# A feed-forward stage with two loading buffers of its own, gate weights loaded singly, and a new order of its first requests

## The reference

```python
def conv_ffn(x, w_up, conv_w, conv_b, w_down):
    h = x @ w_up                                  # 1024 -> 2 * 2816
    h = causal depthwise conv of width 3 over positions, + conv_b
    val, gate = jnp.split(h, 2, axis=-1)
    return (jax.nn.gelu(gate) * val) @ w_down     # 2816 -> 1024
# h = h + conv_ffn(rms_norm(h, norm_ffn_g), ...)
# gate = sigmoid(rms_norm(h, norm_ple_g) @ ple_w_gate)
# h = h + gate * (p @ ple_w_proj);  out = rms_norm(h, final_norm_g)
```

## Time and profile before

| What | Value |
|---|---|
| Median of 3 runs | 2889.82 us (2889.08 to 2893.59) |
| Profiled execution, its own time | 2886.86 us |
| Its span | 2885.3 us |
| Mean granted clock of TensorE | 0.955 of full speed |
| Feed-forward stage | about 1177 to 2605 us of the span |
| First half: up, down | about 1226 to 1659 us, 1659 to 1922 us |
| Second half: up, down | about 1922 to 2346 us, 2346 to 2605 us |

### The profile page before, as it was taken

How to read it: one execution, slowest core, us unless ns; L and a number is a source line. 1 busy time by engine, 2 the same in 40 slices (tenths; PEclk the granted TensorE clock), 3 DMA queues, 4 the chain that set the end, 5 groups by cost and what they waited for, 6 DMA issues and landing times. The chain is left out here.

```text
span 2885.3 us, 38789 instructions
## 1 busy us (share of the span) xinstructions
PE 2607.5 (90%) x13883; PEld 2239.3 (78%) x13883; DVE 1712.4 (59%) x3358; ACT 1368.2 (47%) x2460; POOL 509.6 (18%) x309
## 2 busy tenths in 40 slices
PE   6999997999845799489999999999999998997998
PEld 5989986999834588478888777778888876775876
DVE  1110272777596776488888755578888864444333
ACT  3343332666423666455555444455555542334444
POOL 3454454666300121000000000000000000000000
PEclk9999998999977799789999999999999999998999
DMA  4665456888333253312222366642222246662221
GB/s 163 195 213 172 152 170 157 188 185 185 70 100 126 87 182 129 104 59 88 88 81 75 116 208 232 224 146 88 88 81 75 87 152 245 223 205 99 79 76 46
DMA packets 313909, 392.09 MB, mean 136 GB/s; under 512 B 22161, under 2 KB 222161, under 8 KB 310650
## 3 DMA queue, kind: packets, MB, share of 16 engines
q1 hardware_dynamic: 299850, 341.60, 39.2%
q0 software_dynamic: 13888, 48.25, 4.3%
HBM read 298.59 MB, written 95.33 MB: 137 GB/s over the span
## 5 line engine op out<-in xcount | busy, mean ns | idle before, releaser
L2355 PE MATMUL ffn_bank<-ffn_x,ffn_ring 128*128 128x512 f32 x880 | 346.0, 393 | 19.1 <-DVE ffn_ring L2149 13.6
L2356 PE MATMUL ffn_bank<-ffn_x,ffn_ring 128*128 128x512 f32 x880 | 345.4, 393 | 0.0
L2357 PE MATMUL ffn_bank<-ffn_x,ffn_ring 128*128 128x512 f32 x880 | 345.4, 392 | 0.0
L504 ACT ACTIVATE att_exps<-att_scores,att_part 128x256 f32<-128x256 f32 (+1 forms) x384 | 153.1, 454 | 124.4 <-DVE att_part L475 121.7
L2355 PEld LDWEIGHTS ffn_bank<-ffn_x,ffn_ring 128*128 128x128 f32 x880 | 166.8, 190 | 55.8 <-DVE ffn_ring L2149 9.1
L475 DVE CUSTOM_DVE_ANT_0 att_scores<-att_bank,att_bias 128x256 f32<-128x256 f32 (+1 forms) x384 | 122.5, 363 | 141.3 <-PE att_bank L422 66.1
L2422 POOL DMA_DIRECT2D ffn_act<-ffn_late x88 | 47.6, 541 | 858.7 <-DVE ffn_late L2201 858.7
L2188 DVE SCALAR_TENSOR_TENSOR ffn_strips<-ffn_strips,ffn_taps 128x512 f32<-128x512 f32 x176 | 132.0, 750 | 111.9 <-ACT ffn_strips L1999 111.9
L938 POOL TENSOR_TENSOR in_w_lo<-in_w,in_w_hi 128x2048 fp32r<-128x2048 f32 x36 | 166.0, 4612 | 183.3 <-ACT in_w_hi L821 183.3
L2357 PEld LDWEIGHTS ffn_bank<-ffn_x,ffn_ring 128*128 128x128 f32 x880 | 166.8, 190 | 34.9
L2356 PEld LDWEIGHTS ffn_bank<-ffn_x,ffn_ring 128*128 128x128 f32 x880 | 166.9, 190 | 34.5
(11 more groups left out here) (337 smaller groups left out, 7004.0 us busy)
## 6 DMA issues: line engine op xcount, KB each, us to landing
ffn_w<-in_ffn_w_up SPq DMA_DIRECT2D x88, 512.0 KB, 4.7
ffn_w<-in_ffn_w_down SPq DMA_DIRECT2D x40, 1024.0 KB, 7.1
in_w<-in_w_in SPq DMA_DIRECT2D x36, 1024.0 KB, 6.2
ffn_act<-ffn_late POOLq DMA_DIRECT2D x88, 256.0 KB, 2.7
ffn_sums<-ffn_act SPq DMA_DIRECT2D x88, 256.0 KB, 4.5
ffn_strips<-ffn_act SPq DMA_DIRECT2D x88, 256.0 KB, 4.5
mixed_part<-branch_results SPq DMA_DIRECT2D x16, 792.0 KB, 5.3
z_rows<-in_result SPq DMA_DIRECT2D x80, 128.0 KB, 2.5
```

What stands on the lines that cost most here:

```text
L504: nc.scalar.activation(exps[:, n % RING, m * width:(m + 1) * width], scores[:, n % RING, m * width:(m + 1) * width], ACT.Exp, bias=part[:, ...
L2355: pe.matmul(out[:, :], hi[:, k], x_hi[kind][:, k], start=(k == 0 and fresh), stop=False, skip_group_check=not fresh)
L2356: pe.matmul(out[:, :], hi[:, k], x_lo[kind][:, k], start=False, stop=False, skip_group_check=not fresh)
L2357: mm = pe.matmul(out[:, :], lo[:, k], x_hi[kind][:, k], start=False, stop=(k == KH - 1), skip_group_check=not fresh)
```

## The change

Three things are done in `feed_forward`.

1. **Loading buffers.** Two buffers of their own, `a_raw`, take the activation blocks from DRAM. `load_a(a)` waits until VectorE has subtracted block a - 2 (`a_lo_ready`), whose place it takes, and no longer for TensorE. The waits for the place of the high and low parts move to ScalarE's `split_a`, which now waits for TensorE to be done with block a - 4. SP issues loads two blocks ahead (`RAW = 2`) instead of four; splits stand three blocks ahead (`AHEAD = 3`) instead of two, and three instead of four blocks are split ahead of the first pass. The buffers lie over the place of `tap_rows`, which is used at the opening alone.
2. **Gate weights.** In the second half the eight requests for them go out one behind each of eight units in passes 1 and 2, units with j = 2 left out.
3. **Opening order.** The weights of feature 0 are requested between the rows of group one and those of group two.

```diff
-    AHEAD = 2
+    AHEAD = 3
     RING = 4
+    RAW = 2
-        tap_rows = st.sb("tap_rows", [2 * F, N_TAPS, P])
+        a_raw = [st.sb(f"a_raw{r}", [P, BANK]) for r in range(RAW)]
+        tap_rows = st.over("tap_rows", [2 * F, N_TAPS, P], F32, nc.sbuf_base - RAW * BANK * 4)
-        a_exact = [sums[:, 1], sums[:, 3], plain[:, BANK:2 * BANK], plain[:, 3 * BANK:4 * BANK]]
-        a_loaded = st.sems("a_loaded", RING)
+        a_loaded = st.sems("a_loaded", RAW)
 # SP
             def load_a(a):
...
-                r = a % RING
-                if a >= h * PASSES * F + RING:
-                    wait_feature_done(sp, *divmod(a - RING, F))
-                elif r < 2:
-                    sp.wait_ge(w_lo_ready, operand_count(h, at[h][F - 1, 7]))
-                else:
-                    sp.wait_ge(conv_ready, (h * F + F - 1) * 4)
+                if a >= RAW:
+                    sp.wait_ge(a_lo_ready, a - RAW + 1)
                 sp.wait_ge(act_stored[o % RING], (o // RING + 1) * DMA)
-                sp.dma_start(a_exact[r], act_rows[f][:, col:col + BANK]).then_inc(a_loaded[r], DMA)
+                sp.dma_start(a_raw[a % RAW][:, :], act_rows[f][:, col:col + BANK]).then_inc(a_loaded[a % RAW], DMA)
             load_rows(0, 0)
+            load_w(0)
             load_rows(0, 1)
-            load_w(0)
-                for a in range(first, first + RING):
+                for a in range(first, first + RAW):
                     load_a(a)
...
-                    if h + 1 == HALVES and p == 1:
-                        sp.wait_ge(product_done, HALVES * N)
-                        for part, src, loaded in w_gate_loads:
-                            sp.dma_start(part, src).then_inc(loaded, DMA)
                     for j, fs in enumerate(unit_features):
                         load_w_after(h * UNITS + F + p * PER_PASS + j)
                         for f in fs:
-                            a = (h * PASSES + p) * F + f + RING
+                            a = (h * PASSES + p) * F + f + RAW
...
+                        if h + 1 == HALVES and p in (1, 2) and j != 2 and p * PER_PASS + j < 2 * PER_PASS + 4:
+                            n = (p - 1) * (PER_PASS - 1) + j - (j > 2)
+                            part, src, loaded = w_gate_loads[n]
+                            if n == 0:
+                                sp.wait_ge(product_done, HALVES * N)
+                            sp.dma_start(part, src).then_inc(loaded, DMA)
 # ScalarE
             def split_a(a):
-                r = a % RING
-                act.wait_ge(a_loaded[r], (a // RING + 1) * DMA)
-                nc.scalar.copy(a_hi[r], a_exact[r]).then_inc(a_hi_ready, 1)
+                h, p, f = feature(a)
+                act.wait_ge(a_loaded[a % RAW], (a // RAW + 1) * DMA)
+                if a >= h * PASSES * F + RING:
+                    wait_feature_done(act, *divmod(a - RING, F))
+                elif a % RING < 2:
+                    act.wait_ge(w_lo_ready, operand_count(h, at[h][F - 1, 7]))
+                else:
+                    act.wait_ge(conv_ready, (h * F + F - 1) * 4)
+                nc.scalar.copy(a_hi[a % RING], a_raw[a % RAW][:, :]).then_inc(a_hi_ready, 1)
 # ScalarE and VectorE
-                        for a in range(first, first + RING):
+                        for a in range(first, first + AHEAD):
                             split_a(a)
...
-                            if first + RING <= a < last_of_half(h):
+                            if a < last_of_half(h):
                                 split_a(a)
 # VectorE
-                nc.vector.tensor_tensor(a_lo[r], a_exact[r], a_hi[r].bitcast(F32), ALU.subtract).then_inc(a_lo_ready, 1)
+                nc.vector.tensor_tensor(a_lo[r], a_raw[a % RAW][:, :], a_hi[r].bitcast(F32), ALU.subtract).then_inc(a_lo_ready, 1)
```

## The result

The changed kernel takes 3019.0 us (median of 6 runs, 3015.3 to 3021.5) against 2890.4 us (2886.6 to 2893.6) for the kernel before, measured beside it: ratio 1.0443, interval 1.0430 to 1.0457, 129 us slower. The profiled execution took 3019.0 us around a span of 3017.4. Forecast were 3006 us and +116; the range of 2915 to 3070 holds the result.

What follows compares the result with a forecast made beforehand. TensorE was taken to bound the kernel, apart from 27.6 us of loading costs in the down-projections. The terms 130 - 10 - 8 + 11.5 + 12 + 8 - 27.6 = +116 us on 2889.8 gave 3006 us, range 2915 to 3070.

Steps and rivals of the forecast that it cites:

- Opening, value 0: Opening: moving feature 0's weights ahead of group two's rows changes nothing, since nobody waits; bounds -1 and +3 us.
- The loading buffers, 26.8 us of work for 21.8: Down-projections: a unit's four loads hold two buffers 26.8 us where 21.8 fit, so units take 13.4 us for 10.9.
- B: Down-projections: a unit's block load issued right behind its weights; lands after them, at 7.8 us against 7.2.
- C: Down-projections: the block load after B; lands at 8.4 us, but its subtraction, behind the weights unit, ends at 13.3.
- the short unit: Down-projections: each pass's unit of two features; with the fifth unit 20.7 us for 16.3, 4.4 too long.
- Two sets of down-projections and the way into them: Both stretches of down-projections, 108 us longer, plus 8 us for entering them (4 per half).
- Single gate loads: Second half's down-projections: eight gate-weight loads issued singly cost 1.5 us each, +12 us; bounds 0 and 16.
- The transposes, -8: Down-projections: the 64 transposes for the next half (8.3 us busy) fit into TensorE's waits, -8 us.
- The signs: Trace signs of being right, such as SP waiting for VectorE in nearly all 176 loads and 310 to 330 us stretches.
- Rival A: Down-projections: weights land in 4.9 us, units are 0.6 us too long, +32 us, 2922 us; chance 0.15.
- Rival B: Down-projections: two buffers suffice, no loading wait is left, the 27.6 us come back less 8, 2870 us; chance 0.10.
- Rival C: Down-projections: TensorE's short idles swing its clock, half the time at 1.2 GHz, +48 us, 3054 us; chance 0.12.

Runs made afterwards that it cites:

- the run with the burst: The full change with gate loads together and the opening order as before, so only the two raw buffers differ from the kernel before: 3005.2 us, ratio 1.0398.

## Why the prediction was right

*What bounds it.* Right. The stretch of up-projections kept its length, and the loss lies where the loads close a loop.

*Opening, value 0.* Right: 0.9999 by itself. The stages ahead of the feed-forward part ended 3 us later in this execution, without any edit there; SP's first request of the stage already leaves at 1180.02 us for 1177.04, so the opening has no part in it.

*The loading buffers, 26.8 us of work for 21.8.* Right in mechanism and nearly in size. The weights land 6.9 us after issue (6.8 forecast), B and the weights keep the order of issue, C goes behind the weights unit. The three runs that change this order bring back 79, 93 and 101 us; a third buffer brings back everything. In passes without gate loads, from the second weights request of a pass to its fifth, each comes 13.0 to 14.9 us behind the last (16.3 behind the row loads), and 13.4 were forecast (15.3 with the residual, which does not show as longer). The unit shown above has 14.4: its weights took 8.0 us, not 6.8, the longest of the 20 large ones that leave right behind a block.

Around the short unit the steps come out otherwise. The fifth unit and the short one take 23.9 to 25.1 us together without gate loads, where 20.7 were forecast; the unit behind them takes 11.4 to 11.7 us for 13.4 (13.9 behind row loads). The second row loads of the first half cost nothing like their 6.0 us: the weights left 5 us behind them and landed in 7.4 us, not 10.9. These errors have both signs, and the two passes around those rows last 158.8 us where the prediction's terms give 158.3 (for a pass 22 features of 2.72 us and 16.3 more, and 6.0 for the rows). That the total comes so near is in part luck.

*The sum.* +116 forecast; +129 by the medians, +132.1 by the spans of the two profiled executions. Of the terms:

- Two sets of down-projections and the way into them: 108 + 8 = 116 forecast; +119.8 measured from first to last matmul, the waits on entering among them. Those two were 7.05 and 4.96 us (TensorE timeline of the changed kernel), 12 instead of 8:

```profile
1677.87 0.80 PE L2391 MATMUL ffn_bank<-ffn_ring,ffn_a_late 128*128 128x512 f32 x1 [7.05 <-DVE ffn_a_late L2167]
...
2430.16 0.79 PE L2391 MATMUL ffn_bank<-ffn_ring,ffn_a_late 128*128 128x512 f32 x1 [4.96 <-DVE ffn_a_late L2167]
```

- Single gate loads: +12 forecast against no gate loads at all. No run has two buffers and none of these loads, and the 13.8 us above are single loads against a burst. In the run with the burst the unit behind it takes 16.2 us for the 11.4 to 11.7 of others, so the burst costs some 4.5 us there; with the 8.1 us of the second set the single ones cost some 13 us. That is an estimate from these rows, and near the 12.
- The transposes, -8: they do not only fill waits. TensorE waits ahead of them as well, twice, 7.4 us in all (grouped lines of 1665 to 1985 us):

```profile
L2328 PE MATMUL ffn_bank<-whole_ident,ffn_strips 128*128 128x128 f32 x64 | 9.2, 291 | 7.4 <-issue 4.0 <-DVE ffn_late L2212 3.3
```

- Left out: entering the second half's up-projections. The prediction walked into the down-projections and not out of them. The first weights of the second half stand in the same two-buffer queue of work, and TensorE waits for them 5.81 us, where it waited 1.03 before:

```profile
1990.99 0.79 PE L2359 MATMUL ffn_bank<-tail_shared,ffn_ring 128*128 128x512 f32 x1 [5.81 <-DVE ffn_ring L2153]
```

```profile
1991.00:2010.00 19.00, 19.00 (x72) 15.46 (x73) 14.69 (x24) 6.21 (x12) 0.75 (x1) 0.85 0.33 110
```

  The 19 us behind it have a granted clock of 0.85 and hold 72 matmuls for the 84 that full rate would give. With the longer up-projections of that half (425.9 us for 421.7), this is +9 us, and with the 3 us ahead of the stage it closes the sum: 119.8 + 9 + 3 = 132.

*The signs.* A stretch of down-projections was to take 310 to 330 us: 320 to 323. SP was to wait for VectorE in nearly all of 176 loads: 130; for the others the trace shows no such wait. The 10 us wait of pass 1 is gone: the longest in the second set is 5.2 us. TensorE was to wait 120 to 170 us in all for L2163: 70.5 us for it, 96.2 with the weights unit. That sign was read wrongly, in two ways. I took the whole loss as idle time, but TensorE's busy time took a good part of it: +49 us for the same number of matmuls. In the two sets at most 27 us of this is the lower clock, an estimate: 75.1 us at half rate hold 37.6 us of work, the 20.5 us of before 10.2. Part of the rest is how idle time is counted: a matmul is shown as 0.39 us long while the next starts 0.227 us behind it, so the first bit of every wait is booked as busy. And I named one waiter. Where the short unit brings the next weights early, the block loads are not the last to come, and the unit's own subtraction is:

```profile
1749.36 0.79 PE L2391 MATMUL ffn_bank<-ffn_ring,ffn_a_late 128*128 128x512 f32 x1 [5.03 <-DVE ffn_ring L2161]
```

*Rival A (weights land as when alone, 2922 us).* Did not happen: 6.9 us. Its price was too low besides: the run in which the weights did land in 5.0 us, with C ahead of the weights unit as well, took 2940 us.

*Rival B (two buffers suffice, 2870 us).* Fell. What it says is true of three buffers, 2872.8 us. With it fell the gain that the prediction drew from the Trainium skill (DMA: Bandwidth & Descriptors, Rules for kernel authors): issue a DMA early and wait for it late. The load is no longer tied to TensorE, yet it leaves later, since a buffer is missing. With four buffers it leaves early again, and that kernel is 28 us faster than the one before, as the rule has it.

*Rival C (clock swings, 3054 us).* A small part of it happened. The granted clock of the two sets is 0.93 and 0.95 for 0.99 and 0.97, and TensorE spends 75 us of them at the lower level (matmuls every 0.43 us) for 20 before. The Trainium skill (TensorE: Matmul & The Clock Gate, A second HAM failure mode) tells of such swings in a kernel with many short idles; the trace agrees that the clock falls more often with more waits, but 75 us of 643 is far from the half that the rival assumed. How much of the 129 us it costs by itself was not isolated: where TensorE waits for a load anyway, slower matmuls fill time that was idle. By the estimate above it is at most 27 us in the two sets; how much of that stays open.

## What to carry to other kernels

Before buffers are separated from the place where data is used, add up for one period how long each buffer is held, from the issue of its load to the end of its last reader, and divide by the period: here 26.8 us of holding in a period of 10.9 asks for 2.5 buffers, and in the runs two lose 4% and three gain 0.6%. Count in that holding time every piece of work that stands ahead of the reader in its engine's program, and every larger transfer ahead of the load in its queue; moving one request or one split past them was worth 79 to 101 us. An edit tried beside a starved loop tells nothing of its own worth: against a burst, the single gate loads gave 6 to 8 us, cost 8 to 14 us, or did nothing, by the buffers around them.

## What the runs showed of the hardware

Loads that leave together hold each other up. A 1 MB load issued 0.4 us behind one of 256 KB lands in 6.9 us (median of the 20 such loads, 6.3 to 8.0); with the weights issued some 3 us behind the last load it lands in 5.0 us. The 256 KB load ahead of it takes 4.6 us, and one issued by itself in the same unit (2698.95 us) 3.0. DMA is busy for only half of the time in these stretches (0.52 and 0.49), but this average hides two parts of a unit. First A, the weights and B are in flight (C leaves at 2694.50), then only the blocks C and D (columns as above; the last two are DMA's share and GB/s):

```profile
2688.50:2697.50 9.00, 8.75 (x36) 6.61 (x36) 1.34 (x3) 0.62 (x1) 0.00 (x0) 1.00 0.58 205
2697.50:2702.90 5.40, 3.08 (x13) 2.18 (x12) 3.56 (x4) 3.56 (x4) 0.00 (x0) 1.00 0.14 50
```

And 1 MB of weights with one block issued 0.6 us behind them and none just ahead, from the run that splits a block ahead of the weights unit; they land in 4.8 us:

```profile
2599.90:2604.60 4.70, 4.70 (x23) 3.88 (x22) 3.54 (x6) 0.62 (x1) 0.75 (x1) 1.00 0.74 255
```

So the slow landing is not a full DMA: its engines are busy for 0.58 of those 9 us, at 205 GB/s, and move less than where no block leaves just ahead of the weights (0.74 and 255 GB/s). After it they have little to do until the loop closes (0.14). Why a load ahead slows them was not tested.

The clock fell at single waits far shorter than the 10 us of the earlier trace rows: behind the waits of 7.05, 4.96, 5.81 and 5.03 us shown above the first matmul takes 0.79 or 0.80 us; behind the one of 1.41 us it takes 0.50. The length of the wait alone does not decide: behind one of 1.97 us (1719.93 us in the changed kernel) the granted clock is 0.50, behind one of 2.58 us (2664.11 us) it stays at 1.00. In the kernel with four raw buffers, with 3.9 us of waits in all, both sets of down-projections have a granted clock of 1.00.
